# Expert blocks of 128 rows for one expert each, the seven overflow blocks behind the 32 fixed ones

## The reference

```
    A = T * TOP_K
    flat_e = expert_id.reshape(A)
...
    def expert_block(args):
        xb, e = args
        hid = jax.nn.silu(xb @ w_gate[e]) * (xb @ w_up[e])
        return hid @ w_down[e]
...
    out = jnp.zeros((T, D), jnp.float32).at[tok_pad].add(y.astype(jnp.float32) * w_pad[:, None])
```

## Time and profile before

| what | value |
|---|---|
| median of three runs | 3016.74 us (3012.98 to 3019.17) |
| the profiled execution's own time | 3026.95 us |
| its span, first to last instruction | 3025.0 us |
| outside the span | 1.95 us |
| router stage | about 972 to 1021 us |
| expert stage | about 1021 to 1335 us |
| sum stage | about 1335 to 1382 us |

### The profile page before, as it was taken

The page is one execution under the profiler, slowest core; times in us unless marked ns, Lnnn a source line. Parts: engine busy times, 40 slices in busy tenths (PEclk is TensorE's granted clock), DMA queues, the critical chain, the costliest instruction groups (busy, mean ns, idle before and its releaser), DMA issues. The chain is left out here.

```text
span 3025.0 us, 28672 instructions
## 1 busy us (share of the span) xinstructions
PE 2745.6 (91%) x10136; PEld 1553.2 (51%) x10136; DVE 1469.1 (49%) x3286; ACT 506.7 (17%) x1087; POOL 722.0 (24%) x620
## 2 busy tenths in 40 slices
PE   6999999999998599978979996999989889988888
PEld 3445634446444333324435656888879743333333
DVE  1134401203012322212236459989889987777773
ACT  2033300011001011122026411111122200000004
POOL 0000000000000022210000006654566555555540
PEclk8999999999998699988989898999989989999998
DMA  5101161530212699961210208999999789999982
GB/s 214 56 28 39 68 271 64 198 125 8 83 65 106 261 389 398 392 255 50 84 63 15 93 20 298 400 403 409 415 370 415 266 343 413 414 412 413 413 349 116
DMA packets 142576, 695.23 MB, mean 230 GB/s; under 512 B 20466, under 2 KB 21874, under 8 KB 110578
## 3 DMA queue, kind: packets, MB, share of 16 engines
...
q10 hardware_dynamic: 800, 3.15, 0.3%
...
## 5 line engine op out<-in xcount | busy, mean ns | idle before, releaser
L513 PE MATMUL ps<-hT,pm_coef_table 128*128 128x256 f32 (+1 forms) x2432 | 507.4, 371 | 30.4 <-DVE hT L439 24.4
L2537 PE MATMUL ps<-hT 128*128 128x512 f32 x1024 | 457.9, 602 | 50.7 <-DMA hT<-in_peer_v 29.4
L2390 POOL DMA_INDIRECT wring<-in_peer_u,pm_rows x256 | 336.9, 1316 | 683.9 <-DVEq L2759 463.0
L513 PEld LDWEIGHTS ps<-hT,pm_coef_table 128*128 128x128 f32 x2432 | 444.5, 192 | 87.5 <-issue 25.1
L513 PE MATMUL ps<-hT,wring 128*128 128x512 f32 (+2 forms) x976 | 412.2, 583 | 10.4 <-PEq L678 2.8
L2390 POOL DMA_INDIRECT wring<-in_peer_v,pm_rows x256 | 319.4, 1248 | 246.0 <-DVE h_tok L2810 207.1
L2810 DVE SCALAR_TENSOR_TENSOR h_tok<-wring,pm_coef,h_tok 128x1024 f32<-128x1024 f32 x256 | 324.3, 1281 | 106.3 <-DMA wring<-in_peer_v,pm_rows 105.0
L2537 PEld LDWEIGHTS ps<-hT 128*128 128x128 f32 x1024 | 190.4, 191 | 317.6 <-issue 226.7
L2643 DVE CUSTOM_DVE_ANT_0 wring<-wring,pm_coef_table 128x1024 f32<-128x1024 f32 x256 | 303.2, 1217 | 40.2 <-DMA wring<-in_peer_u,pm_rows 39.6
L513 PEld LDWEIGHTS ps<-hT,wring 128*128 128x128 f32 (+1 forms) x976 | 185.1, 191 | 231.6 <-issue 229.8
L1579 POOL COPY ex_idx<-row_token 128x1 uint32 (+1 forms) x24 | 4.4, 183 | 1153.7 <-PEq L1711 1021.3
...
## 6 DMA issues: line engine op xcount, KB each, us to landing
...
```

The costliest lines, as they stand in the source:

```text
L513: mm = env.nc.tensor.matmul(out, w[:, k, lo:hi], rhs(k), start=(k == 0), stop=(k == KD - 1))
L2390: nc.gpsimd.indirect_dma_start(ring[n % RING], None, dram[name], bass.IndirectOffsetOnAxis(ap=rows[:, t, j:j + 1], axis=0)).then_inc(got[n ...
L2537: mm = nc.tensor.matmul(env.ps[:, OUT[k], :], W[n % 2][:, at:at + P], vr[p % 2][:, m % 2 * D + k % 2 * WBLK:m % 2 * D + (k % 2 + 1) * WBLK ...
```

## The change

`EB` becomes 128: each block has one expert, 128 rows and the full width of the array. There are 32 fixed blocks and `LATER` = 7 overflow blocks, `NB` = 39 blocks in all, and `ORDER` runs them by number, so the overflow blocks come last. The hardware loops become straight code. The rings hold 6 blocks of gate and up weights and 4 of down weights; 16 MB of them are issued in the router stage. Row numbers are read from `row_token` and `row_place` directly, `x` has 4 buffers and `y` 3 (two and one of them in the new tile `ex_rows`). A result goes to row `k * S + token` of `y_dram`, so `y_dram` has 1024 rows, all written, and is no longer preset. The upper four feature slices are made on ACT, the down products are evacuated on DVE, which multiplies them by the gate there. In the sum stage plain DMAs on SP read the rows, and DVE adds them with two instructions per tile in place of three and one on ACT. The diff, without renames and small steps:

```diff
@@ -1027,8 +1027,6 @@
                     nc.sync.dma_start(R.qdec[:, hd], row).then_inc(R.qdec_in[hd], 16)
                 nc.sync.dma_start(R.band[:], dram["ret_band"]).then_inc(R.band_in, 16)
                 load_blocks(env, sp, until=b_v[1] + 1)
-                nc.sync.dma_start(dram["y_dram"].rearrange("(b p) d -> p b d", p=P),
-                                  env.gates[:, 0, :].unsqueeze(1).broadcast_to([P, NB, D])).then_inc(env.y_set, 16)
                 load_blocks(env, sp)
...
@@ -1349,15 +1347,14 @@
 
 ROWB = P
 PICKS = 2
-EB = P // 2
-LATER = (PICKS * S - PICKS) // EB + 1
-NEB = NE + LATER
-NB = NEB // 2
+EB = P
+LATER = (PICKS * S - 1) // EB
+NB = NE + LATER
 SLOT = 2
-LAST = NB // SLOT
-TRIPLES = LATER // 2
-GUS = 3
-ROUND = 6
+GUS = 6
+DNS = 4
+XS, YS = 4, 3
+ORDER = list(range(NB))
 UNUSED = 8192.0
 GUW = KD * 2 * EF
...
+            @block.gpsimd
+            def _(pool):
+                nc.gpsimd.memset(E.more_rows[:], 0.0)
...
-                         (row_no, "row_numbers"), (block_no, "block_numbers"), (tok_no, "token_numbers"),
-                         (place, "row_places"))
+                         (row_no, "row_numbers"), (block_no, "block_numbers"), (tok_no, "token_numbers"))
                 for dst, name in loads:
                     nc.sync.dma_start(dst[:], dram[name]).then_inc(in_s, 16)
-                for h in range(2):
-                    nc.sync.dma_start(E.gu[0][h], dram["experts"][h, :, 0:GUW]).then_inc(E.gu_got[0], 16)
-                for h in range(2):
-                    nc.sync.dma_start(E.dn[0][h], dram["experts"][h, :, GUW:]).then_inc(E.dn_got[0], 16)
-                for n, h in ((1, 0), (2, 1)):
-                    nc.sync.dma_start(E.gu[n][h], dram["experts"][n + 1, :, 0:GUW]).then_inc(E.gu_got[n], 16)
-                    if n == 1:
-                        nc.sync.dma_start(E.dn[n][h], dram["experts"][n + 1, :, GUW:]).then_inc(E.dn_got[n], 16)
+                for b in range(GUS):
+                    nc.sync.dma_start(E.gu[b], dram["experts"][ORDER[b], :, 0:GUW]).then_inc(E.gu_got[b], 16)
+                    if b < DNS:
+                        nc.sync.dma_start(E.dn[b], dram["experts"][ORDER[b], :, GUW:]).then_inc(E.dn_got[b], 16)
                 load_blocks(env, sp)
...
-                fixed_e = block_e[:, 0:NE].rearrange("p (g n) -> p g n", n=4)
-                later_e = block_e[:, NE:NEB].rearrange("p (g n) -> p g n", n=2)
-                order = order_e[:].rearrange("p (g n) -> p g n", n=6)
-                step(v, [V.tensor_copy(order[:, :, 0:3], fixed_e[:, :, 0:3]),
-                         V.tensor_copy(order[:, :, 5:6], fixed_e[:, :, 3:4]),
-                         V.tensor_copy(order[:, :, 3:4], later_e[:, :, 1:2]),
-                         V.tensor_copy(order[:, :, 4:5], later_e[:, :, 0:1])])
-                step(v, [V.tensor_copy(E.block_expert[:], order_e[:])])
+                step(v, [V.tensor_copy(E.block_expert[:], block_e[:])])
                 product_done(env, v, t_rows)
-                lo, hi = slice(0, EB), slice(EB, P)
-                pairs = in_pair[:].rearrange("p (g n) -> p g n", n=3)
-                fixed = env.ps[:, t_rows[0], 0:NE // 2].rearrange("p (g n) -> p g n", n=2)
-                later = env.ps[:, t_rows[0], NE // 2:NB].unsqueeze(2)
-                step(v, [V.tensor_copy(pairs[:, :, 0:1], fixed[:, :, 0:1]),
-                         V.tensor_copy(pairs[lo, :, 1:2], fixed[lo, :, 1:2]),
-                         V.tensor_copy(pairs[hi, :, 2:3], fixed[hi, :, 1:2]),
-                         V.tensor_copy(pairs[lo, :, 2:3], later[lo])])
-                V.tensor_copy(pairs[hi, :, 1:2], later[hi]).then_inc(env.bank_free[t_rows[0]], 1)
...
+                V.tensor_copy(in_pair[:], env.ps[:, t_rows[0], 0:NB]).then_inc(env.bank_free[t_rows[0]], 1)
...
+        x = [spare[:, s * D:(s + 1) * D] for s in range(SLOT)] + [E.more_rows[:, s, :] for s in range(XS - SLOT)]
+        y = [spare[:, (SLOT + s) * D:(SLOT + s + 1) * D] for s in range(SLOT)] + [E.more_rows[:, XS - SLOT, :]]
...
-                def gather(i, s):
-                    b = SLOT * i + s
-                    pool.wait_ge(rows_full, 2 * b + 2)
-                    pool.nop(nofuse=True)
-                    nc.gpsimd.tensor_copy(idx[:, s:s + 1], E.row_token[:, bass.ds(b, 1)]).then_inc(idx_s, 1)
...
+                def gather(b):
+                    if b >= XS:
+                        pool.wait_ge(rows_full, 2 * (b - XS) + 2)
+                    nc.gpsimd.indirect_dma_start(x[b % XS], None, dram["xn_dram"], bass.IndirectOffsetOnAxis(
+                        ap=E.row_token[:, ORDER[b]:ORDER[b] + 1], axis=0), bounds_check=S - 1,
+                        oob_is_err=False).then_inc(x_got[b % XS], 16)
...
+                for b in range(XS + 2):
+                    gather(b)
+                for b in range(NB):
+                    if b + XS + 2 < NB:
+                        gather(b + XS + 2)
+                    scatter(b)
...
+                for b in range(GUS, NB):
+                    sp.wait_ge(gu_full, b - GUS + 1)
+                    load(E.gu[b % GUS], b, 0, GUW, gu_got[b % GUS])
+                    down(b - DNS + 1)
+                for b in range(NB - DNS + 1, NB):
+                    down(b)
...
-                        for h, r in enumerate(rows_of):
-                            mm = nc.tensor.matmul(env.ps[r, GU[s], :], xT[:, s, k, r], wg[n % GUS][h][:, k, :],
-                                                  start=(k == 0), stop=(k == KD - 1))
+                        if k % HALF_K == 0:
+                            pe.wait_ge((xT_low, xT_high)[k // HALF_K], b + 1)
+                        mm = nc.tensor.matmul(env.ps[:, GU[s], :], xT[:, s, k, :], wg[b % GUS][:, k, :],
+                                              start=(k == 0), stop=(k == KD - 1))
...
-                            for h, r in enumerate(rows_of):
-                                mm = nc.tensor.matmul(env.ps[r, DOWN[q], :], hidT[:, s, k, r],
-                                                      wd[s][h][:, k, q * WBLK:(q + 1) * WBLK],
-                                                      start=(k == 0), stop=(k == EFT - 1))
+                            mm = nc.tensor.matmul(env.ps[:, DOWN[q], :], hidT[:, s, k, :],
+                                                  wd[b % DNS][:, k, q * WBLK:(q + 1) * WBLK],
+                                                  start=(k == 0), stop=(k == EFT - 1))
...
+                for b in range(NB):
+                    if b + 1 < NB:
+                        gate_up(b + 1)
+                    hidden(b)
+                    if b + 2 < NB:
+                        rows(b + 2)
+                    down(b)
...
-                    for n in range(2):
-                        act.wait_ge(dn_full, 2 * b + n + 1)
-                        nc.scalar.activation(y[:, s, n * WBLK:(n + 1) * WBLK], env.ps[:, DOWN[n], :],
-                                             ACT.Copy).then_inc(y_done, 1)
...
+                def high_features(b):
+                    act.wait_ge(rows_full, 2 * b + 2)
+                    for j in range(HALF_K):
+                        k = HALF_K + j
+                        ins = nc.scalar.activation(xT[:, b % SLOT, k, :], env.ps[:, ROWS[1], j * P:(j + 1) * P],
+                                                   ACT.Identity, scale=gain(k), bias=shift(k))
+                    ins.then_inc(xT_high, 1)
...
+                def gated(b):
+                    if b >= YS:
+                        v.wait_ge(y_out[b % YS], 16 * (b // YS))
+                    for q in range(2):
+                        cs = slice(q * WBLK, (q + 1) * WBLK)
+                        v.wait_ge(dn_full, 2 * b + q + 1)
+                        nc.vector.tensor_tensor(y[b % YS][:, cs], env.gates[:, 1, cs], env.ps[:, DOWN[q], :],
+                                                ALU.mult).then_inc(y_done, 1)
...
+                picked = dram["y_dram"].rearrange("(k t p) d -> t p k d", k=PICKS, p=P)
                 nc.sync.dma_start(pT[:], dram["p_T"]).then_inc(p_in, 16)
                 nc.sync.dma_start(wp[:], dram["w_ple_proj"]).then_inc(p_in, 16)
+                nc.sync.dma_start(y[:, 0], picked[0]).then_inc(got[0], 16)
                 nc.sync.dma_start(row[:], dram[row_name].broadcast_to([P, D])).then_inc(row_in, 16)
+                for t in range(1, NT):
+                    nc.sync.dma_start(y[:, t], picked[t]).then_inc(got[t], 16)
...
-                for t in range(NT):
-                    for k in range(PICKS):
-                        nc.gpsimd.indirect_dma_start(y[:, t, k, :], None, dram["y_dram"], bass.IndirectOffsetOnAxis(
-                            ap=E.pos[:, k, t:t + 1], axis=0)).then_inc(got[t], 16)
...
-                def first(t):
-                    act.wait_ge(got[t], 16 * PICKS)
-                    nc.scalar.activation(y[:, t, 0, :], y[:, t, 0, :], ACT.Copy, scale=E.weight[:, 0, t:t + 1]).then_inc(first_s, 1)
...
```

(18 more changed lines are left out.)

310 lines of the change are left out of this document (112 added, 198 removed).

## The result

The changed kernel takes 3164.34 us (median, 3162.5 to 3166.12), the kernel before 3017.14 us beside it (3012.98 to 3019.17). The ratio is 1.0487, with a 95% interval of 1.0473 to 1.0501: slower by 147 us. The forecast was 3166 us. The profiled execution took 3163.24 us, its span is 3161.1 us.

The account below looks back on a forecast made before the run. PE was taken to bound the kernel. Expert periods +165, start -6, end -3 and sum stage -7 made +149 us on 3016.7, so 3166 us; own range 3155 to 3184, 8-in-10 range 3150 to 3192.

Parts of the forecast that it names:

- The bound: Expert stage: PE sets the pace, busy 258.7 of 262 us; the transfers, DMA 0.95 busy, just keep up.
- A block's cost and the count: Expert stage: 39 full-width blocks of 11.45 us replace 24 pairs; +165.0 us, bounds +163.2 and +174.0.
- The start: Expert stage's start: copies gone, first gather landing sooner, shorter feature waits; -6 us, bounds -3 to -10.
- The end: Last scatter to next stage: copy ahead of it gone, quicker landing; -3 us, bounds -1 to -5.5.
- The sum stage: Sum stage: DVE adds tiles as they arrive, first square and later tiles earlier; -7 us, bounds -3 and -10.
- The preset: Mixer: removing the 12 MB store saves 0 us, since it is hidden under an unbroken 82.56 us of PE work.
- (1): Rival, new waits inside each block: 3186 us at 0.5 us per block, 3205 at 1 us; chance 0.10.
- (2): Rival, PE's granted clock falls from 1.00 to 0.95 in the expert blocks: 3189 us; chance 0.04.
- (3): Rival, more comes back than counted, empty overflow blocks freeing the DMA engines earlier: 3145 to 3155 us; chance 0.07.
- (4): Rival, not slower: transfers set the expert stage's pace and full-width blocks are cheap for PE; 3017 us, chance 0.01.
- (5): Rival, most overflow blocks are skipped and cost nothing: 80 us less, 3086 us; chance 0.02.
- The signs: Expected in the changed kernel's trace: gate_up period 11.40 to 11.50 us, PE at 100%, first transposes at 1026 to 1031 us.

Follow-up runs that it names:

- order_between: Changed kernel with overflow blocks placed between the fixed ones, from the second group of four on, instead of last: 3166.89 us, ratio 1.0487 to the kernel before.
- half_width: Changed kernel with gate_up and down products cut to the first 64 stationary columns, instruction count kept: 3175.24 us, ratio 1.0520 to the kernel before.
- late_preload: Changed kernel with 10 MB of expert weights issued in the router stage, the other 6 MB at the expert stage's start: 3171.76 us, ratio 1.0502.
- plus_first: The kernel before's two-expert pairs with the change's other parts, an added GpSimd drain and SyncE waiting for first rows before 5 MB of weights: 2997.59 us, ratio 0.9927.
- with_preset: Changed kernel with the 12 MB preset of the result table put back in the mixer: 3166.07 us, ratio 1.0485 to the kernel before.
- only_fixed: Changed kernel with the seven overflow blocks left out, 32 passes: 3084.97 us, ratio 1.0218 to the kernel before.

## Why the prediction was right, point by point

**The bound.** Right. PE was full before and is fuller after; no wait for expert weights is left, and the overflow blocks' place changes nothing (order_between).

**A block's cost and the count.** Right, and it is the whole answer: 36 periods of 11.394 us for 21 of 11.77, +163.0 for the +165.0 predicted. The 2 us between them is one step: I let the 0.27 us between the 2 and the 8 transposes stay, "between equal shapes". It became 0.22 us, and 0.27 to 0.28 is what half_width brings back; it was part of the price of the changing shapes. The bound of 11.40 was the true value. As a rule for that price I had named mode switching in the Trainium skill (TensorEngine Tiling (Array Packing), Key Properties), which says that it drains TensorE. half_width shows a price where the shapes meet, 0.30 us for a block with two runs of 128*64 among transposes of 128*128; that a drain is what takes this time, no run shows.

**The start.** -10.7 in place of -6, just outside the bound of -10. The step that was mis-sized is the landing of the first gather. I gave it -2 in 0 to -5.6, "since the end of the 16 MB is close to the gather"; it was -5.8. The windows show the 16 MB at 427 GB/s in 975 to 1000 us, where I had reckoned with the 372 of before, which is 10.7 MB by 1000; the 5.6 MB of the next window (281 GB/s in 20 us) end near 1013 at that pace, some 4 us ahead of the gather and not at 1021. Finer windows bear this out: 451 GB/s in 1010 to 1012 us, nothing at all in 1014 to 1018. late_preload and plus_first show both directions. The waits for features went from 1.97 + 2.29 to 0.70 + 1.12 us, -2.4 in place of -2. The other -0.9 of the piece, which the forecast didn't have, is the shorter period (-0.3) and the first `gate_up`, from start to the next step 9.98 us before and 9.44 after (-0.5); the granted clock was 0.50 in 1021 to 1036 us before and 0.69 in 1020 to 1035 us after.

**The end.** Wrong in sign: +1.7 in place of -3. I took the 7.4 us between the last scatter and the next stage for the landing of the scatter. The row itself said otherwise: its idle time was ended by POOLq L1572, the stage's closing line, not by a DMA. Of the 7.4 us, 2.4 were the rest of the transfer, 4.0 the drain and 1.0 the release. The scatter did get quicker, and the copy ahead of it did go: from the last `down` to the drain it is 8.4 us in place of 8.9. But 30 more transfers made the drain 2.5 us longer, and that is what the stage's end now has.

**The sum stage.** -8.3 in place of -7, within its bounds. The square of the first tile starts 10.62 us after the stage's first product instead of 15.83, -5.2 (predicted -5.4); the remaining tiles gave -3.1 in place of -2.4. DVE, in the changed kernel, timeline:

```profile
1495.18 2.60 DVE L1817 SCALAR_TENSOR_TENSOR h_tok<-es_y,pick_weight,h_tok 128x1024 f32<-128x1024 f32 x2 [20.89 <-DMA es_row<-in_norm_final]
1499.19 2.60 DVE L1817 SCALAR_TENSOR_TENSOR h_tok<-es_y,pick_weight,h_tok 128x1024 f32<-128x1024 f32 x2 [1.41 <-DMA es_y<-y_dram_out]
```

**The preset.** 0, as predicted (with_preset).

**The rivals.** (1) and (2) did not come: in the whole stage PE waited 1.8 us for features and 1.1 us ahead of the last two `down`, and the clock was 1.00 from 1048 to 1470 us. (3) was half true: more came back at the start and in the sum stage, less at the end. (4), the one on the other side, needed blocks of 7.8 us on average, the empty ones at 5.6 or less; they took 11.39. (5), overflow blocks without cost, is out by only_fixed: they cost 79.4 us. The sum came to +145.4 in the traces where +149 was forecast. Against the forecast the terms are off by -2.0 (periods), -4.7 (start), +4.7 (end), -1.3 (sum stage) and -0.4 (last `gate_up` to last `down`): two errors of 4.7 us cancel, so the total stands better than its parts. That part of the closeness is luck; the main term, +163.0 for +165.0, is not.

**The signs.** Right were PE at 100% with the clock at 1.00, DMA at 0.69 and then 0.07, and nearly the sum stage of about 41 us (1484.9 to 1524.35, 39.5). The period was 11.39 us, just under the 11.40 to 11.50. Two signs failed, and they belong to the two terms that were most off, the start and the end: PE's first transposes came at 1021.7 and not at 1026 to 1031 (this execution was 3.7 us ahead when the router began, which doesn't explain it all), and from the end of the last down product (1473.6) to the next stage (1484.9) it was 11.3 us and not 6 to 8.
